# A hybrid mLSTM and GLA layer on one core: final norm squared feature-major, forget-gate projection stacked in rows, level stages moved by one or two pieces

## The reference

```python
h = _rmsnorm(x, g_norm1) * (1.0 + scale1) + shift1
z = h @ w_in                                   # all projections of both mixers
# mixer A: mLSTM; mixer B: gated linear attention with a log forget gate per key channel
la = (jax.nn.log_sigmoid((lr_b @ w_alpha + b_alpha)) / GLA_TAU)       # lr_b has 16 columns of z
b = jnp.cumsum(lc, axis=2)
A = jnp.einsum('bhtd,bhsd,bhtsd->bhts', qc, kc, exp(b_t - b_s))       # causal, inside a chunk
y = (sigmoid(g_a) * ha + sigmoid(g_b) * hb) @ w_out
x = x + gate1 * y
h2 = _rmsnorm(x, g_norm2) * (1.0 + scale2) + shift2
x = x + gate2 * ((silu(h2 @ w_ffn_gate) * (h2 @ w_ffn_up)) @ w_ffn_down)
y_prompt = _rmsnorm(xp, g_final); y_sample = _rmsnorm(xs, g_final)    # x * rsqrt(mean(x*x)) * g_final
```

## Time and profile before

| | |
|---|---|
| median of 3 runs | 1947.8 us (1945.98 to 1949.23) |
| profiled execution, its own time | 1946.25 us |
| its span, first to last instruction | 1944.5 us |
| mean granted TensorE clock | 0.988 of full |
| PE busy | 1896.1 us, 98% |
| DVE, ACT, POOL busy | 1059.8, 682.1, 683.4 us |
| DMA | 155.07 MB, mean 80 GB/s |

### The profile page before, as it was taken

The page is one execution under the profiler, slowest core; times in us unless marked ns, Lnnn a source line. Parts: engine busy times, 40 slices in busy tenths (PEclk is TensorE's granted clock), DMA queues, the critical chain, the costliest instruction groups (busy, mean ns, idle before and its releaser), DMA issues.

```text
span 1944.5 us, 33250 instructions
## 1 busy us (share of the span) xinstructions
PE 1896.1 (98%) x13205; PEld 1812.6 (93%) x13205; DVE 1059.8 (55%) x1900; ACT 682.1 (35%) x1425; POOL 683.4 (35%) x582
## 2 busy tenths in 40 slices
PE   7899999999999999999999999998999999999997
PEld 4899999999999989999899999998999999999996
DVE  5731554414553236534174578786756666566657
ACT  4523424334233243342343554322232223322333
POOL 3211332312232212313132484334454345444541
PEclk8999999999999999999999999999999999999999
DMA  9241221322222322214223553111121112111212
GB/s 337 70 100 50 74 78 54 112 77 69 76 61 69 108 76 71 56 61 128 58 82 108 176 156 98 44 34 55 44 66 42 46 44 66 50 39 44 66 44 101
DMA packets 211266, 155.07 MB, mean 80 GB/s; under 512 B 10196, under 2 KB 195732, under 8 KB 210600
## 3 DMA queue, kind: packets, MB, share of 16 engines
q1 hardware_dynamic: 210810, 152.73, 26.5%
q10 hardware_dynamic: 302, 0.22, 0.0%
HBM read 131.42 MB, written 21.50 MB: 79 GB/s over the span
## 4 chain that ended last, share of the span: by engine, by line
PE 87%; DVE 6%; issue 2%; POOL 2%; ACT 1%; DMA 1%; DVEq 0%; ACTq 0%; SPq 0%; POOLq 0%
PE bank L919 35%; PE bank L2073 19%; PE bank L2042 13%; PE bank L1963 3%; PE bank L1004 3%; PE bank L1930 2%; PE bank L1022 2%; PE bank L1024 1%; PE bank L1027 1%; PE bank L955 1%; PE bank L1065 1%; DMA w_ada_ring<-in_w_ada 1%; PE bank L942 1%; PE bank L1054 1%; DVE y_rows L2646 1%
## 5 line engine op out<-in xcount | busy, mean ns | idle before, releaser
L1264 POOL TENSOR_TENSOR w_lo<-w_raw,w_hi 128x512 fp32r<-128x512 f32 x128 | 180.7, 1412 | 713.8 <-ACT w_hi L1087 713.8
L919 PE MATMUL bank<-h_hi,w_hi 128*128 128x352 f32 x1536 | 328.8, 336 | 1.4 <-ACT w_hi L1087 1.4
L919 PE MATMUL bank<-h_hi,w_lo 128*128 128x352 f32 x1536 | 313.5, 326 | 1.2 <-POOL w_lo L1264 1.1
L919 PE MATMUL bank<-h_lo,w_hi 128*128 128x352 f32 x1536 | 312.8, 325 | 0.0
L919 PEld LDWEIGHTS bank<-h_hi,w_hi 128*128 128x128 f32 x1536 | 257.0, 190 | 16.6 <-issue 12.1
L919 PEld LDWEIGHTS bank<-h_hi,w_lo 128*128 128x128 f32 x1536 | 260.4, 190 | 2.7 <-POOL w_lo L1264 2.7
L919 PEld LDWEIGHTS bank<-h_lo,w_hi 128*128 128x128 f32 x1536 | 260.4, 190 | 0.0
L2286 POOL TENSOR_TENSOR f_lo<-w_raw,f_hi 128x512 fp32r<-128x512 f32 x107 | 143.5, 1346 | 201.1 <-ACT f_hi L2111 201.1
L2286 POOL TENSOR_TENSOR w_lo<-w_raw,w_hi 128x512 fp32r<-128x512 f32 x107 | 143.5, 1347 | 153.0 <-ACT w_hi L2111 153.0
L2623 DVE SCALAR_TENSOR_TENSOR x_t<-bank,ada,x_t 128x352 f32<-128x352 f32 (+1 forms) x288 | 156.0, 567 | 56.3 <-PE bank L2042 38.8
L1087 ACT ACTIVATE w_hi<-w_raw 128x512 fp32r<-128x512 f32 x128 | 80.2, 626 | 166.2 <-PE bank L919 166.1
(11 more groups left out here) (480 smaller groups left out, 3861.3 us busy)
## 6 DMA issues: line engine op xcount, KB each, us to landing
w_raw<-in_w_in SPq DMA_DIRECT2D x128, 256.0 KB, 2.9
w_ada_tile<-in_w_ada SPq DMA_DIRECT2D x32, 512.0 KB, 4.3
w_raw<-in_w_out SPq DMA_DIRECT2D x48, 256.0 KB, 2.9
w_raw<-in_w_ffn_gate SPq DMA_DIRECT2D x44, 256.0 KB, 3.0
w_raw<-in_w_ffn_up SPq DMA_DIRECT2D x44, 256.0 KB, 3.0
w_raw<-in_w_ffn_down SPq DMA_DIRECT2D x44, 256.0 KB, 2.8
w_ada_ring<-in_w_ada SPq DMA_DIRECT2D x8, 1024.0 KB, 7.8
x_scratch<-x_turned_rows SPq DMA_DIRECT2D x1, 4224.0 KB, 13.8
```

What stands on the lines that cost most here:

```text
L919: last = pe.matmul(g.ps[b][:, 0:n], x[:, s, k, :], y[:, 4 * h + k, c0:c0 + n], start=(h == 0 and k == 0 and m == 0), stop=(h == 1 and k == ...
L1264: pool.tensor_tensor(Wl[:, s], raw[:, r], Wh[:, s].bitcast(F32), ALU.subtract).then_inc(s_lo, 1)
```

## The change

Three parts are changed. First, `alpha` becomes one fp32r product of 80 rows for each third: rows 0 to 15 hold the upper parts of both factors, rows 32 to 47 the lower part of the inputs with the upper of the weights, rows 64 to 79 the upper of the inputs with the lower of the weights. The rows are prepared once, in stages `alpha_hi` and `alpha_lo` of the first window A; `rows` moves into the memory of `v_b`. Second, the last norm: ACT squares each piece of `x_t` as soon as DVE has added it and then scales it by `g_final` (now a column for each feature), POOL adds up the squares, DVE adds the last ones, PE sums over the features with a column of ones, and the turned rows need one scaling, half by DVE and half by ACT. Third, numbers in `AT_SLOT` move level stages.

```diff
-    "A": [("decay", 1), ("ada_load0", 2), ("scores", 6), ("keys", 6), ("interq", 8),
+    "A": [("decay", 1), ("ada_load0", 2), ("alpha_hi", 3), ("alpha_lo", 9), ("scores", 6), ("keys", 6), ("interq", 8),
...
-          ("silu_q", 10), ("ada0", 14), ("level3", 14), ("ada_load1", 15), ("level4", 16), ("vt0", 16), ("conv_k", 20),
-          ("level5", 20), ("level6", 22), ("ada1", 22), ("taps_k", 24), ("level7", 26), ("adas0", 27), ("ada_load2", 27), ("vt1", 27),
+          ("silu_q", 10), ("ada0", 13), ("level3", 13), ("ada_load1", 15), ("level4", 15), ("vt0", 15),
+          ("level5", 18), ("conv_k", 20), ("level6", 22), ("ada1", 22), ("taps_k", 24), ("level7", 26), ("adas0", 27), ("ada_load2", 27), ("vt1", 27),
...
-          ("level5", 6), ("gate_r0", 7), ("ada_load1", 8), ("level6_k", 8), ("level6", 8), ("level7", 10), ("ada1", 11),
+          ("level5", 6), ("gate_r0", 7), ("ada_load1", 8), ("level6", 9), ("level7", 11), ("ada1", 11),
...
                     elif name == "alpha":
-                        for b, (c0, m) in enumerate(PARTS):
-                            full(pe.matmul(use(n + b)[:, 0:m], wal[64:64 + RANK, i * DK:(i + 1) * DK], rows[64:64 + RANK, c0:c0 + m], start=True, stop=True))
+                        pe.wait_ge(s_rows, 4)
+                        for c in range(NPC):
+                            c0, m = span(c)
+                            full(pe.matmul(use(n + c)[:, 0:m], wal[0:64 + RANK, i * DK:(i + 1) * DK], xal[0:64 + RANK, c0:c0 + m],
+                                           start=True, stop=True))
...
+            turn(0)
+            mean_squares(0)
+            turn(1)
+            mean_squares(1)
+            turn(2)
+            mean_squares(2)
+            for t in range(3, NT):
+                turn(t)
...
+                act.activation(dst, X[:, n, c0:c0 + w], ACT.Square).then_inc(s_sq, 1)
...
+                act.activation(X[:, n, c0:c0 + w], X[:, n, c0:c0 + w], ACT.Copy, scale=gain[:, n:n + 1]).then_inc(s_fs, 1)
...
+            for k in range(NPC, NPC * (KC - 1)):
+                c0, w = span(k % NPC)
+                m = k - NPC
+                pool.wait_ge(s_sq, 24 + k + 1)
+                if m >= NPC:
+                    pool.wait_ge(s_sqa, 18 + m - NPC + 1)
+                pool.tensor_tensor(SQX[:, c0:c0 + w], SQX[:, c0:c0 + w], SQR[m % NSQ], ALU.add).then_inc(s_sqa, 1)
...
+            for c in range(NPC):
+                last_sum(c)
+            for c in range(NPC):
+                inverse_of(c)
+                if c < 2:
+                    left_half(c)
+            for t in range(2, NT):
+                left_half(t)
```

More of the change, by code:

```diff
@@ L1174, in window @@
                         act.wait_ge(s_rows, 1)
+                    elif name == "alpha_hi" and i == 0:
+                        act.wait_ge(s_r3, 1)
+                        for r in (0, 64):
+                            act.activation(xal[r:r + RANK, :], rows[64:64 + RANK, :], ACT.Copy)
+                        for r in (0, 32, 64):
+                            last = act.activation(wal[r:r + RANK, :], w_rows[r:r + RANK, :], ACT.Copy)
+                        last.then_inc(s_rows, 1)
+                    elif name == "alpha_lo" and i == 0:
+                        act.wait_ge(s_rows, 3)
+                        act.activation(xal[32:32 + RANK, :], rows[64:64 + RANK, :], ACT.Copy)
+                        act.activation(wal[64:64 + RANK, :], w_rows[64:64 + RANK, :], ACT.Copy).then_inc(s_rows, 1)
                     elif name in ("silu_q", "silu_k"):
@@ L1194, in window @@
                     elif name == "alpha":
[L1195 to L1198, removed]
+                        for c in range(NPC):
+                            c0, m = span(c)
+                            wait_use(act, w, i, n + c)
+                            last = act.activation(QD[:, c0:c0 + m], RB(n + c)[:, 0:m], ACT.Copy)
+                            last.then_inc(free(n + c), 1)
                         act.wait_ge(s_nab, i + 1)
@@ L2088, in _, with mean_squares, turn @@
             lastp = Place("down", NBLK - 1)
[L2089 to L2092, removed]
-                n = P if t < NC else NS
+            def mean_squares(c):
+                pe.wait_ge(s_fm, c + 1)
+                if c < 2:
+                    bnk, turns = lastp.piece(22 + c)
+                    pe.wait_ge(s_pf[bnk], turns + 1)
+                else:
+                    pe.wait_ge(s_rt, NPC + 1)
+                for t in DONE_WITH[c]:
+                    n = P if t < NC else NS
+                    last = pe.matmul(MS[c][0:n, t:t + 1], SQX[:, t * P:t * P + n], one, start=True, stop=True)
+                last.then_inc(s_sum, 1)
+            def turn(t):
+                n = P if t < NC else NS
+                pe.wait_ge(s_fs, 3 * (KC - 1) + third(t) + 1)
+                if t >= NE:
+                    pe.wait_ge(s_fo, t - NE + 1)
+                    pe.wait_ge(s_smh, t - NE + 2)
+                else:
+                    for k in (16 + 2 * t, 17 + 2 * t):
+                        bnk, turns = lastp.piece(k)
+                        pe.wait_ge(s_pf[bnk], turns + 1)
                 for b in range(2):
-                    if t >= NE and b == 0:
-                        pe.wait_ge(s_fo, t - NE + 1)
                     for k in range(4):
@@ L2266, in _ @@
             run(act, step)
-            for t in range(NT + 1):
-                n = P if t < NC else NS
[L2269 to L2278, removed]
+            lastp = Place("down", NBLK - 1)
@@ new lines, in last_gain @@
+            def last_gain(k):
+                n, c = divmod(k, NPC)
+                c0, w = span(c)
+                act.wait_ge(s_sq, 24 + k + 1)
+                if k == 0:
+                    act.wait_ge(s_gf, 16)
+                act.activation(X[:, n, c0:c0 + w], X[:, n, c0:c0 + w], ACT.Copy, scale=gain[:, n:n + 1]).then_inc(s_fs, 1)
+            act.activation(fss[:, NT - 1, 3:4], eps, ACT.Sqrt)
+            late = NPC * (KC - 1)
+            for k in range(NPC * KC):
+                if k == late:
+                    last_gain(k - 1)
+                last_square(k)
+                if k >= late:
+                    last_gain(k)
+                elif k:
+                    last_gain(k - 1)
@@ new lines, in root_of, with right_half @@
+            def root_of(c):
+                act.wait_ge(s_sum, NPC + c + 1)
+                t0, t1 = DONE_WITH[c][0], min(DONE_WITH[c][-1] + 1, NC)
+                last = act.activation(RT[:, t0:t1], MS[c][:, t0:t1], ACT.Sqrt, bias=eps[:, :], scale=1.0 / D)
+                if c == NPC - 1:
+                    last = act.activation(RT[0:NS, NC:NT], MS[c][0:NS, NC:NT], ACT.Sqrt, bias=eps[0:NS, :], scale=1.0 / D)
+                last.then_inc(s_rt, 1)
+            def right_half(t):
+                n = P if t < NC else NS
+                act.wait_ge(s_fr, third(t) + 1)
+                act.wait_ge(s_ft, 2 * t + 2)
+                if t == 0:
+                    act.wait_ge(s_out, 16 * 4)
+                if t >= NXR:
+                    act.wait_ge(s_y[t % NXR], 16 * (t // NXR))
+                act.activation(OT[0:n, t % NXR, 512:1024], ENDB[2 * (t % NE) + 1][0:n, :], ACT.Copy, scale=RI[0:n, t:t + 1]).then_inc(s_smh, 1)
@@ L2652, in _ @@
             dve.memset(eps[:, :], EPS)
+            dve.memset(one, 1.0)
             dve.memset(fss[:, :, :], 1.0)
             run(dve, step)
[L2655 to L2663, removed]
+            for c in range(NPC):
+                last_sum(c)
+            for c in range(NPC):
+                inverse_of(c)
+                if c < 2:
+                    left_half(c)
+            for t in range(2, NT):
+                left_half(t)
 class Shared:
```

83 lines of the change are left out of this document (66 added, 17 removed).

## The result

The changed kernel takes 1960.45 us (median of 4 runs, 1959.95 to 1966.61) where the kernel before takes 1947.58 (4 runs). The ratio is 1.0071, with a 95% interval of 1.0058 to 1.0084: slower by 0.7%, some 13 us. The forecast was 1951.2 and its range ended at 1957.5.

A forecast was written before the change was run, and what follows sets the result against it. PE, busy 1896.1 of 1944.5 us, was taken as the bound. Alpha -8.4, end -4.5, moved levels +11.8 and clock +4.6 gave +3.5 on 1946.25: 1949.7, or 1951.2 on the runs' scale; range 1939.5 to 1957.5.

The forecast's parts named there:

- The moved levels: Windows B and L: PE waits for keys queued behind POOL's `w_lo`, +10.1 in three windows B, +1.75 in L, together +11.8 us.
- The end: Last norm: POOL's additions set the first store, then stores set the pace; -4.5 us, from -3.5 to -5.5.
- Alpha in all -8.4: Forget-gate product in four heads: -5.8 shorter product, -3.9 avoided clock falls, +1.3 level 0 waits; between -5.4 and -9.7 us.
- +1.3: Level 0 behind `alpha`: PE arrives sooner by more than DVE's chain does, so waits for `q_decayed` grow, +1.3 us together.
- slack of 1.55: Second head, level 0: `q_decayed` ready at 477.58, PE arrives at 479.13, leaving a wait of 0.2 to 0.3 us after the change.
- -3.9: Clock falls behind `alpha` in heads 1 to 3 go with the slow fp32 product, 3 x 1.3 us; the less certain half.
- -5.8: `alpha` product itself: about 1.95 us on the path becomes 0.49, four heads by 1.46 us.
- no slack: First head, level 0: PE's longest wait for `q_decayed`, 1.0 us, is there, so its wait grows by 0.44.
- 3 to 4 new falls: PE's clock behind new waits at seven places (levels 4, 5 and 6): falls of 1.3 us each, +4.6, from 0 to 10.
- The one on the other side: Rival: moved levels cost nothing because `w_lo`'s buffer is freed one piece sooner; about 1932.9 to 1935 us, chance 0.12.
- Nearly every place falls: Rival: 6 to 8 clock falls cost 8 to 10 us, one at `alpha` stays in some head; 1955 to 1959, chance 0.13.

The follow-up runs named there:

- e4: The kernel before with the moved level stages alone: 1964.32 us, ratio 1.0094.
- e5: The kernel before with the new end (last norm) alone: 1942.83 us, ratio 0.9965.
- e1: The changed kernel with the level stages back at their old slots; new forget-gate product and new end stay: 1942.74 us, ratio 0.9974.
- e6: The kernel before with the new forget-gate product (`alpha` and its stages) alone: 1948.60 us, ratio 0.9999.
- e9: e1 with POOL making only 8 of 512 columns of the `w_lo` at slot 39 of each window A: 1933.31 us, ratio 0.9919.
- e2: The changed kernel with POOL's keys of levels 4, 5 (windows B) and 6 (window L) one slot earlier, ahead of `w_lo`: 1935.80 us, ratio 0.9939.
- e3: e1 with DVE's `gate0` in window A moved from slot 36 to slot 40, behind level 0: 1929.56 us, ratio 0.9906.
- e7: e5 (old forget-gate product) with `gate0` moved behind level 0, to slot 40: 1941.74 us, ratio 0.9957.

## Why the prediction missed

**The moved levels: right.** It gave +11.8 us of waits. Measured: 1.46 + 2.08 - 0.47 - 0.22 = 2.85 a window B, 8.6 for three, and 1.73 in window L: 10.3. Level 4 was 1.46 for 1.5 forecast, level 5 2.08 for 2.3, level 6 1.73 for 1.75; level 3 showed no wait (0.25). With its falls the part was put at 11.8 + 4.6 = 16.4. e4 says 0.0094 x 1948.25 = 18.3, by its median 16.1.

**The end: right in place, low in size.** -4.5 with -3.5 to -5.5; e5 says -6.8 by its ratio, -5.3 by its median. POOL's addition took 16.36 / 18 = 0.91 us, not 1.02, but from its end to the first store it is 3.5 us, not 2.2, so that the first store comes 3.3 us earlier where 2.6 was said. What came on top is behind the first store: 13.0 us in e1, not 14.3. The term had the stores set that pace, by the 13.8 us of the transfer to `x_scratch`; the runs show 12.8 to 14.8 where PE's clock stays up until they are nearly out, and 16.1 in the two profiles where it doesn't. The changed kernel's is one of them, and gained only 3.4 in all.

**Alpha: the step that failed.** "Alpha in all -8.4" was 0 (e6). The product itself did what it was to do: 1.46 us a head, and no fall behind it. The stages `alpha_hi` and `alpha_lo`, put at nothing, cost nothing: from the first piece to the first `alpha` it is 139.1 us before and 139.2 after. Two of its terms were wrong. First the "+1.3" for level 0: the slack of 1.55 was right, and so was a chain that begins about 1.1 sooner, but `q_decayed` was carried over at 0.68. Moved against POOL's `w_lo`, it grew by 1.07, so that the wait was 1.47 in all four heads: 4 x 1.47 - 0.99 = +4.9. The text even had the row that shows such holding (L2634, 0.19 to 1.07) and used it for the end alone. e9 shows that this is the cause: without that `w_lo` the wait is 0.42, near the forecast 0.2 to 0.44. Second the "-3.9" for the falls behind `alpha`. It was taken as a gain of 1.3 a head, with no effect on the wait but an earlier PE. In the kernel before, e4 and e5, all with the old product and gate0 ahead of level 0, the eight heads with the fall don't wait at level 0 and have `q_decayed` at 0.68; the four without it wait 0.98 or 0.99 and have it at 1.76. So a fall saved was worth some 0.3 us (1.3 less the 0.99, an estimate) and not 1.3, even before the product changed. And the falls came back at level 0, behind its new waits: -5.8 + 4.9 leaves -0.9, and e6's profile has 27.3 us at half clock (6.8 of them at 96 us, ahead of any `alpha`) where the kernel before has 13.6.

The first head was there to be read before the change: the prediction took its wait of 1.0 for a head with "no slack" and did not look at what made it, a `q_decayed` of 1.76 beside POOL.

By parts the prediction was -8.4 + 16.4 - 4.5 = +3.5; the parts alone measured 0 + 18.3 - 6.8 = +11.5 (by medians +0.5 + 16.1 - 5.3 = +11.3), and the whole +13. The miss is the alpha term nearly alone; levels and end were off by about 2 us each and nearly cancel, which is luck.

**Clock: the number of falls, not the price.** 3 to 4 new falls was the guess. The profile after has four stretches behind levels 4 and 5 in the windows B (284.8, 298.5, 557.9, 820.7), a new one behind level 6 of window L (1066.5, beside the old one behind level 5), three behind level 0, and the one at 1339.6; three of them are 6.8 us long. A fall of 3.4 us still let 13 or 14 matmuls through, which costs 1.1 to 1.3. In the profiled execution nine more times 3.4 us make some 12 us; 10.3 + 4.9 - 5.8 - 3.4 + 12 = 18 of the 20.4. The remaining 2 us are already there at the first piece, which starts at 65.1 us, before at 63.2. The profiles differ there by as much among themselves (62.7 in e6, 66.1 in e5), so they are not put down to a part. The median has 6 us less than the profile, and where is not shown; the end at half clock could be 3 us of it.

**Rivals.** The one on the other side, that `w_lo` isn't in the way, fell with e1 and e4. "Nearly every place falls" (1955 to 1959) was the nearest of them, and still 1.5 us short, as it kept the gain of alpha.

## What to carry to other kernels

When an edit makes one engine earlier, price the chain that it now waits for with its neighbours at their new places: the duration of an instruction read beside an idle POOL does not hold beside a busy one. The same holds for a loss that is to be removed: the falls behind `alpha` kept POOL's `w_lo` behind `q_decayed`, and without them it stood ahead. A stage that stands behind a preparation for the next buffer inherits that preparation's wait; here it was enough to move the keys one slot up (e2). And test the parts in pairs: the product and gate0's place were worth nothing and 1 to 2 us each, and over 10 us together.

## What the runs showed of the hardware

- DVE's `gate` took 1.26 us with POOL idle (e3), and 2.22 beside POOL (changed kernel, e9); POOL's `w_lo` goes from 1.28 to 2.28. Eight columns on POOL took 1.23, to 0.07 behind the end of DVE's `gate` (e9).
- In the changed kernel's profile PE waits 1.46 to 2.08 us at twelve levels, and the clock fell behind nine of them (not behind level 0 of the first head, nor level 4 of the second and third). Behind a wait of 0.98 or 0.99 at level 0 it fell once in four (e4 first head; not in the kernel before), and behind none of the waits of 0.42 and 0.47 in e3 and e9.
- The falls behind the slow fp32 `alpha` are not fixed to it: four heads in e5, three in the kernel before, one each in e4 and e7, with the same product. What decides this was not tried.
- With PE's clock up, 8 stores left in 8.4 us and the span ended 13.0 us behind the first (e1); with it down, 12.0 and 16.1 (changed kernel and e9).
